# Start addresses of the SBUF tiles in a two-layer decoder kernel: residues of 128 and 416 against multiples of 2048 bytes

## What is computed

```python
for i in range(DEPTH):
    y = swa_sink_attention(x, ...) if i % 2 == 0 else forgetting_attention(x, ...)
    x = layer_norm(ALPHA * x + y, ln_g[i, 0], ln_b[i, 0])
    y = conv_ffn(x, ffn_w_up[i], ffn_conv_w[i], ffn_conv_b[i], ffn_w_down[i])
    x = layer_norm(ALPHA * x + y, ln_g[i, 1], ln_b[i, 1])
```

## Time and profile before

| | |
|---|---|
| median of 3 runs | 2227.64 us (2227.63 to 2227.85) |
| the profiled execution | 2227.25 us |
| its span (first to last instruction) | 2225.4 us |
| TensorE busy in the span | 2194.1 us, 99% |
| weight loads of TensorE busy | 2027.2 us, 91% |
| VectorE, ScalarE, GpSimd busy | 1336.2, 1039.6, 219.6 us |
| mean granted TensorE clock | 0.996 of full |

### The profile page before, as it was taken

The page is one execution under the profiler, slowest core; times in us unless marked ns, Lnnn a source line. Parts: engine busy times, 40 slices in busy tenths (PEclk is TensorE's granted clock), DMA queues, the critical chain, the costliest instruction groups (busy, mean ns, idle before and its releaser), DMA issues.

```text
span 2225.4 us, 40894 instructions
## 1 busy us (share of the span) xinstructions
PE 2194.1 (99%) x15265; PEld 2027.2 (91%) x15265; DVE 1336.2 (60%) x1805; ACT 1039.6 (47%) x1380; POOL 219.6 (10%) x206
## 2 busy tenths in 40 slices
PE   8999999999999999999999999999999999999996
PEld 7998899999999988888899998899999999988885
DVE  5566576666666554446665665576666566654445
ACT  4554365454545443335444444364545454543332
POOL 2000002310000000000240330001230000000001
PEclk9999999999999999999999999999999999999998
DMA  8444556666666655555655654656666666665553
GB/s 262 152 149 157 180 163 206 199 198 188 187 186 187 187 188 188 189 186 158 189 183 163 203 172 140 196 160 196 201 203 187 188 188 188 186 225 187 187 188 104
DMA packets 206952, 408.71 MB, mean 184 GB/s; under 512 B 12652, under 2 KB 13756, under 8 KB 206620
## 3 DMA queue, kind: packets, MB, share of 16 engines
q1 hardware_dynamic: 200192, 385.92, 56.5%
q0 software_dynamic: 5776, 21.34, 3.1%
q10 hardware_dynamic: 908, 0.43, 0.1%
HBM read 405.46 MB, written 2.18 MB: 183 GB/s over the span
## 4 chain that ended last, share of the span: by engine, by line
PE 94%; DVE 3%; DMA 1%; ACT 1%; issue 0%; SPq 0%; ACTq 0%; DVEq 0%
PE ps L1176 19%; PE ps L1179 18%; PE ps L1178 18%; PE ps L1162 11%; PE ps L1164 11%; PE ps L1163 11%; PE ps L1304 1%; PE ps L1311 1%; DVE w_lo L749 1%; PE ps L1322 1%; PE ps L1323 1%; PE ps L1303 1%; PE ps L1321 0%; DMA raw<-in_a_w_qkv_dram 0%; DMA raw<-in_b_w_qkvf_dram 0%
## 5 line engine op out<-in xcount | busy, mean ns | idle before, releaser
L749 DVE TENSOR_TENSOR w_lo<-raw,w_hi 128x1024 fp32r<-128x1024 f32 x728 | 924.4, 1276 | 662.5 <-ACT w_hi L471 662.0
L471 ACT ACTIVATE w_hi<-raw 128x1024 fp32r<-128x1024 f32 x728 | 771.6, 1060 | 989.0 <-PE ps L1179 550.5
L1176 PE MATMUL ps<-xh,w_lo 128*128 128x256 f32 x3572 | 1006.3, 282 | 2.4 <-DVE xl L790 1.7
L1179 PE MATMUL ps<-xh,w_hi 128*128 128x256 f32 x3572 | 996.2, 279 | 0.0
L1178 PE MATMUL ps<-xl,w_hi 128*128 128x256 f32 x3572 | 996.2, 279 | 0.0
L1176 PEld LDWEIGHTS ps<-xh,w_lo 128*128 128x128 f32 x3572 | 671.7, 188 | 5.4 <-DVE xl L790 3.1
L1178 PEld LDWEIGHTS ps<-xl,w_hi 128*128 128x128 f32 x3572 | 671.9, 188 | 0.4
L1179 PEld LDWEIGHTS ps<-xh,w_hi 128*128 128x128 f32 x3572 | 671.4, 188 | 0.0
L1164 PE MATMUL ps<-w_hi,hid_h 128*128 128x512 f32 x704 | 278.4, 396 | 0.0
L1162 PE MATMUL ps<-w_lo,hid_h 128*128 128x512 f32 x704 | 278.4, 396 | 0.0
L1163 PE MATMUL ps<-w_hi,hid_l 128*128 128x512 f32 x704 | 278.4, 396 | 0.0
(11 more groups left out here) (164 smaller groups left out, 1501.1 us busy)
## 6 DMA issues: line engine op xcount, KB each, us to landing
raw<-in_ffn_w_up_dram SPq DMA_DIRECT2D x352, 512.0 KB, 3.6
raw<-in_ffn_w_down_dram SPq DMA_DIRECT2D x176, 512.0 KB, 4.4
raw<-in_b_w_qkvf_dram SPq DMA_DIRECT2D x96, 512.0 KB, 4.2
raw<-in_a_w_qkv_dram SPq DMA_DIRECT2D x40, 512.0 KB, 4.3
raw<-in_a_w_o_dram SPq DMA_DIRECT2D x32, 512.0 KB, 4.5
raw<-in_b_w_o_dram SPq DMA_DIRECT2D x32, 512.0 KB, 4.6
bias<-rel_by_distance POOLq DMA_DIRECT2D x4, 1024.0 KB, 6.6
bias<-minus_cumulated_decay POOLq DMA_DIRECT2D x4, 1024.0 KB, 6.8
```

Source lines behind the costliest of these rows:

```text
L471: act.activation(w_hi[:, loc % RING], raw[:, loc % RING], ACT.Copy).then_inc(high_ready, 1)
L749: dve.tensor_tensor(w_lo[:, s], raw[:, s], w_hi[:, s].bitcast(FP32), ALU.subtract).then_inc(low_ready, 1)
L1176: pe.matmul(o, w_lo[:, slot, k % 2, cols], xh[:, k, :], start=(k == 0 and j % 2 == 0), stop=False, skip_group_check=True)
L1179: last = pe.matmul(o, w_hi[:, slot, k % 2, cols], xh[:, k, :], start=False, stop=(k == KT - 1), skip_group_check=True)
```

## The change

Ten small tiles and `warm` come first, then a filler, then the large tiles, with `convcol` and a second filler ahead of `xh`. No instruction is added, removed or moved; each keeps its shape, its order and its waits, and only SBUF addresses differ.

```diff
-        res = sb("res", [P, MT, D])
-        raw = sb("raw", [P, RING, 2, COLS])
-        w_hi = sb("w_hi", [P, RING, 2, COLS], F32R)
-        w_lo = sb("w_lo", [P, RING, 2, COLS], F32R)
-        tok = sb("tok", [P, MT, COLS])
-        cg = sb("cg", [P, 4, SEQ])
-        cu = sb("cu", [P, 4, SEQ])
-        lnp = sb("lnp", [P, 2, COLS])
         ident = sb("ident", [P, P])
         lncol = sb("lncol", [P, 2, DEPTH, 2, KT])
-        convcol = sb("convcol", [P, DEPTH, 4, 2 * FT])
         cw = sb("cw", [P, 2, 4, 4])
...
         warm = sb("warm", [P, 1])
+        sb("fill_to_res", [P, (1920 - 1592) // 4])
+        res = sb("res", [P, MT, D])
+        raw = sb("raw", [P, RING, 2, COLS])
+        w_hi = sb("w_hi", [P, RING, 2, COLS], F32R)
+        w_lo = sb("w_lo", [P, RING, 2, COLS], F32R)
+        tok = sb("tok", [P, MT, COLS])
+        cg = sb("cg", [P, 4, SEQ])
+        cu = sb("cu", [P, 4, SEQ])
+        lnp = sb("lnp", [P, 2, COLS])
+        convcol = sb("convcol", [P, DEPTH, 4, 2 * FT])
+        sb("fill_to_xh", [P, 320])
         with ExitStack() as first:
             xh = sb("xh", [P, KT, SEQ], F32R, first)
```

## The result

The changed kernel takes 2239.47 us (2239.15 to 2240.58, five runs) against 2227.64 before (2227.31 to 2227.85). The ratio is 1.0054, with a 95% interval of 1.0039 to 1.0068: 11.8 us slower, over twice the 4.5 us that the prediction took as what a measurement can tell from no change. The profiled execution took 2239.63 us with a span of 2237.8, so 12.4 us more than the span of before.

The account below looks back on a forecast made before the run. The prediction took TensorE's matmul pace to bound the kernel. To 2227.25 us it added 0 for TensorE's operands, VectorE and ScalarE, loads and small tiles, forecasting 2227.6 us for the timed median, range 2223.0 to 2232.0.

Parts of the forecast that it names:

- The bound: Whole kernel: time is the sum of its matmuls, TensorE busy 2194.1 of 2225.4 us, six projection lines 88% of the chain.
- The zero for TensorE's operands: Projection matmuls: moving operand addresses changes 0 us, since crossing and non-crossing slices and different offsets stream at one rate.
- The equal cost per column: Both projection forms: 0.456 ns per column for 256 and 512 columns, so the loss is proportional to columns.
- VectorE, ScalarE, loads: Elementwise operations and weight loads: 0 us; bounds 2 ns in 1049 per operation and 2 us either side for loads.
- the rival in which only loads gain: Weight loads: 1 to 2 us gained, 2225.6 to 2226.6 us, within no change; part of the 0.80.
- The slower one: Every projection matmul: stationary and moving reads fall into step, up to 3.4 ns each, up to 2275 us; chance 0.08.
- Its argument against itself: Score matmuls: both operands at 416, in step, 215 ns each against 213, so at most 2 ns; called no proof.
- The faster rival: TensorE operands: round addresses recover the lost tenth, 2047 us in full, 2210 for a tenth of it; chance 0.12.
- The range: Whole kernel: 2223.0 to 2232.0 us, around 2227.6 plus or minus 3.7, leaving out most of both rivals.
- The bounds of this term: TensorE's operands: 181 us gained if the whole excess goes, 48 us lost if the larger weight load is paid twice.
- the chance on zero: Whole kernel: no change, 2227.6 us, given chance 0.80.

Follow-up runs that it names:

- e9: Of the change only res and raw stay at 0 modulo 2048, weights back at 128 and activations at 416 as before; 2227.09 us against 2227.79 before, ratio 0.9997.
- e1: Changed kernel with xh and all behind it back at 416 modulo 2048, weights at 0; 2239.80 us, ratio 1.0049 to the kernel before.
- e6: Each weight ring slot followed by 64 unused bytes, activations at 128, so operand start distances of 0, 448, 384, 320 modulo 512 for turned matmuls; 2238.68 us.
- e7: Each weight ring slot followed by 64 unused bytes, activations at 384, so operand start distances of 256, 192, 128, 64 modulo 512; 2238.25 us.
- e3: Changed kernel with other filler sizes, so that weights and activations both start at 128 modulo 2048; 2240.36 us, ratio 1.0058 to the kernel before.
- e11: Weight ring slots padded by 64 bytes, weights 16 bytes into their slots, operand start distances 48, 240, 176, 112 modulo 256; 2244.16 us.

## Why the prediction was wrong

**The bound.** Right: TensorE's pace is the time. 88% of the chain is in six lines before, 90% after, and two distances times two counts give the change to 0.9 us.

**The zero for TensorE's operands.** This step failed. It found crossing and non-crossing slices, and operands at 128 and at 416, at one rate, and took that as "addresses don't matter". But within the kernel before the distance between the two operands modulo 256 is one number, 32, for both forms of projection matmul: every block and slice inside a tile starts at a multiple of 512 from the tile's start. These rows could not vary what counts. The changed kernel has 0 for both, and the term measured +35.7 - 22.4 us; the net of 13.3 is small because the two forms went opposite ways.

**The equal cost per column.** 0.456 ns in both forms was read as a rate of the array's supply. It was a coincidence of phase 32. At a granted clock of 0.5 the starts of matmuls with 512 columns lie 426 or 427 ns apart, before as after (four distances take 1.70 us in both), so 1.2 columns per ns. An estimate from this, for twice the clock, is 2.4 columns per ns, which the prediction names a column per cycle of 2.4 GHz (the traces give the clock as a share alone): 106.7 and 213.3 ns. Over that the matmuls lose 10.0 and 20.0 ns before, 13.3 and 13.3 after. At phase 0 the loss is the same per matmul in both forms, and the rows of before hold no projection matmul at phase 0 that could have shown it.

**VectorE, ScalarE, loads.** Right. They stayed within 4 ns an operation, against a bound of 2, and e9 puts what the loads' landing place is worth at 0.9997 (0.9988 to 1.0006). That interval runs from 2.7 us less to 1.3 us more, so the 1 to 2 us of the rival in which only loads gain are neither shown nor excluded.

**The rivals.** The slower one, at 0.08, named the right quantity, the distance between the two operands; its picture of two reads in step is not shown. It gave a price of up to 3.4 ns from the decay projection's rows, and for 256 columns it was 3.33. That is luck: 3.4 was read as the price of a larger load, but the decay projection runs at other phases (64 and 192 in turn), and in e1 and e9 the same small loads go with 120.0 ns. The rival was also wrong in two points: it put the same price on the 512 columns, which gained 6.67 instead, so it said 2275 where 2239.5 came; and it took a modulus of 512 where e6 and e7 show 256 to be enough. Its argument against itself, score matmuls in step at no cost, was drawn from plain float32 matmuls, each of which stands in the trace as two records with starts 0.22 us apart (64 score matmuls with 256 columns, 128 records of L1304); the 0.43 us are one such matmul. No run asked whether they can collide. The faster rival had a piece of truth, 6.67 ns for 512 columns, for another reason than round addresses (e3). The 106.3 ns that it hoped for did not come up as the pace of any run; with full loads the lowest was 116.7.

The runs speak against an independence of the two operands: the pace of the same streams moved from 116.7 to 120.0 with their phase, and by 1.1 and 2.2 ns when a load (and with it the output) was cut.

**The range.** The bounds of this term (181 us down, 48 up) were kept out of the range because the chance on zero was 0.80. With the mechanism unmeasured in either direction that was too much.

## What to carry to other kernels

Where float32r matmuls set the time, the start addresses of weights and activations are a knob: take the distance of starts from the timeline for each form of matmul, then shift one tile by a filler of 32 to 224 bytes and read it again. What counts most is the difference of the two operands' starts modulo 256, and each form has its own best value (of 16 tried, 32 for 256 moving columns with 116.7 ns, 0 for 512 with 226.7), so tiles that serve different forms want different residues; a round address showed no worth of its own (e3, with none, has the changed kernel's 120.0 and 226.7 ns; e9, with `res` and `raw` round, ratio 0.9997). Read the pace in every stage, since at some phases (48, 112, 160) it differed between two stages with the same loop, by 3.1, 1.5 and 1.4 ns for 256 columns. And a loss that is alike in all rows of a kernel is not shown to be unavoidable, if all its rows share the quantity that might cause it.

## What the runs showed of the hardware that was not expected

- The distance of starts of float32r matmuls at the full clock depends on the difference of the two operands' start addresses, with a period of 256 bytes (e6 and e7 agree, 0 and 128 differ): 116.7 to 120.0 ns with 256 columns and 226.7 to 234.6 with 512.
- With the same addresses and the same loop it can still settle at different values (118.7 and 117.3 ns in e1 and, at phase 48, 119.9 and 116.8 in e11, in layers 0 and 1; 113.3 ns before and 120.0 in e9 in the decay projection, at the same residues).
- Cutting the weight load and the output of one matmul of three to 32 of 128 columns brings both layouts to 117.8 ns, which is 2.2 ns less for one and 1.1 ns more for the other.
- VectorE (1218 ns before, 1218 and 1219 after) and ScalarE (1049 and 1047 ns before, 1045 and 1043 after) on 1024 elements per partition don't show the start addresses of their tiles by more than 4 ns.
